# The last 30 expert rows of v: all through TensorE's diagonal matmuls, none added by VectorE into the residual

## The chip, the cores and the metric

The kernel runs on one core of one Trainium2 chip. The metric is the device time of one launch in microseconds (us), lower is better. The engines are TensorE (PE in the profile, its weight loads are PEld), VectorE (DVE), ScalarE (ACT), GpSimd (POOL) and SyncE (SP). The profile is of one execution on the same core.

## The reference, cut to what matters

The program is three layers long: a convolution mixer, a sparse-attention mixer, and a third block that ends in a mixture of 16,384 tiny experts. The change lies in the last part of that third block. For each of 512 tokens and 8 heads, 16 experts are picked. Each has a row in `peer_u` (dotted with the token) and a row in `peer_v` (added with a weight into the token's output).

```python
def peer_ffn(h, w_q, sub_keys, u, v):
    ...
    g = jax.nn.softmax(top_s, axis=-1)
    def one_block(args):
        xb, ib, gb = args
        ue = jnp.take(u, ib, axis=0)
        a = jnp.einsum('thkd,td->thk', ue, xb, preferred_element_type=jnp.float32)
        w = jax.nn.gelu(a) * gb
        ve = jnp.take(v, ib, axis=0)
        return jnp.einsum('thk,thkd->td', w.astype(ve.dtype), ve)
...
x = x + peer_ffn(rmsnorm(x, norm_ffn[i]), peer_wq[i], peer_subkeys[i], peer_u[i], peer_v[i])
g_ple = jax.nn.sigmoid(rmsnorm(x, norm_ple[i]) @ ple_gate[i])
x = x + g_ple * (p[i] @ ple_proj[i])
```

All data is f32. The last two lines are the closing stage, called ple below: it needs the finished sum over all expert rows of its tokens.

## The kernel before, in words

The 512 tokens are four blocks of 128, one token to a partition. A block and a head make a group; there are 32 groups of 16 picks, so 512 picks. One pick (a "row" below) is one gather of 128 different rows of 1024 f32, 0.5 MB, by GpSimd's indirect DMA: one from `peer_u` (line 1567, tile G) and one from `peer_v` (line 1583, tiles H and XT). Both kinds go out on GpSimd's one queue, in program order: u and v gathers take turns until the u gathers end, and then the v gathers left over (480 to 511) follow one another. The groups are ordered so that block 3's come last; rows 384 and above, and so all that the change touches, belong to block 3.

**u.** VectorE dots each u row with the token's normalized input (line 2246). When the 16 dots of a group are there it makes the weights together with ScalarE: `activated` (lines 2160 to 2162), `weigh` on ScalarE (lines 1433 and 1434), `weighted` (lines 2168 to 2171).

**v through TensorE.** For row v ScalarE scales the identity by the 128 weights of that pick (`diagonal`, line 1446), into one of 8 diagonal buffers in MK. TensorE multiplies this diagonal by the gathered row, in two halves of 512 columns, and accumulates in the block's two PSUM banks (`expert_row`, line 1017). The profile has four matmul records for such a row, two for each half. The end of the second half raises `v_done`. ScalarE's order puts `weigh` of the last group ahead of the diagonal of row 480.

**v through VectorE.** A row for which `by_vector(v)` is true (line 170) skips the diagonal and TensorE. VectorE adds weight times row into the residual X (`add_row`, line 2179), once it is through with the last group's weights, and raises `v_added`. With V_LATE = 482 these are rows 482, 485, ..., 509: 10 of the last 30.

**Buffers of v.** From row 96 on there are 8 row buffers, used in turn: 4 in H (`v_loaded0` to `3`) and 4 in XT (`v_loaded4` to `7`). The gather of row v waits until row v - 8 has been consumed, on `v_done` or on `v_added`, whichever engine consumed it (lines 1577 to 1581). `by_tensor(v)` and `vector_rows(v)` count the rows up to v that each engine takes; the waits and the diagonal's buffer number follow from them.

**The closing stage of block 3.** `ple_sum` on VectorE waits for `v_done` of row 511 and adds the two banks to X (line 2187). TensorE transposes (line 1079), ScalarE and VectorE scale and copy (lines 1455, 2193), TensorE runs the gate's matmuls (line 1091), ScalarE takes the sigmoid (line 1463), VectorE multiplies and adds (lines 2211, 2212), and SyncE stores (line 514). The projection of block 3 (line 1106, 8 records) stands in TensorE's order ahead of row 499.

Of the kernel before, what the change touches and what calls it, by code (L numbers as in the profile page):

```python
# [47 lines left out]
V_LATE = PICKS - 30  # L48
# [120 lines left out]

def by_vector(v):  # L170

    return v >= V_LATE and v % 3 == 2


def vector_rows(v):

    return sum(by_vector(a) for a in range(v + 1))


def by_tensor(v):  # L180

    return sum(not by_vector(a) for a in range(v + 1))
# [7 lines left out]
def program(nc, x, xT, mem, wstream, fmvec, rows, norm_rows, consts, levels, subkeys, pT, proj, peer_u, peer_v, out):  # L190
    with ExitStack() as ctx:
# [327 lines left out]
        def _(pe):  # L519
# [486 lines left out]
            def expert_row(v):  # L1006
                if by_vector(v):
                    return
                n, k = v // PEER_K, v % PEER_K
                b = group(n)[0]  # L1010
                if v == 0:
                    pe.wait_ge(tail_free, made)
                at, uses = v_place(v)
                pe.wait_ge(diag_full, by_tensor(v))
                pe.wait_ge(v_loaded[at], 16 * uses)
                for half in range(2):
                    mm = pe.matmul(ps[2 * b + half][:, :], DG[by_tensor(v - 1) % DIAG_RING], VB[at][:, half * T:(half + 1) * T],  # L1017
                                   start=(n == FIRST[b] and k == 0), stop=(n == LAST[b] and k == PEER_K - 1),
                                   skip_group_check=True)
                mm.then_inc(v_done, 1)  # L1020
# [1328 lines left out]
```

## Time and profile before

| what | value |
|---|---|
| time, median of 3 runs | 3289.33 us |
| the three runs | 3283.68, 3296.66, 3289.33 us |
| span of the profiled execution | 3278.9 us |
| TensorE busy | 2812.3 us, 86% |
| VectorE busy | 1829.2 us, 56% |
| GpSimd busy | 1273.9 us, 39% |
| mean granted TensorE clock | 0.967 |

The profiled execution's own time, with launch and end around the span, is not listed apart; its span lies 10.4 us below the median of the runs. The rows' gathers fill the last part of the span: in 16 of the last 17 of the page's 40 slices the DMA engines move 345 to 387 GB/s, and in the last 15 slices TensorE is busy 6 to 8 tenths.

### The profile page before, as it was taken

How to read it: one execution, taken by the hardware profiler on the slowest of the kernel's cores; microseconds unless marked ns; L12 is line 12 of the kernel's file. 1: busy time of each engine (PE TensorE's matmuls, PEld its weight loads, DVE VectorE, ACT ScalarE, POOL GpSimd, SP SyncE). 2: the span in 40 equal slices, each digit the busy share in tenths (PEclk: the TensorE clock that was granted, in tenths of full speed). 3: DMA queues.
4: the chain of work that ended last, by engine and by line, in shares of the span. 5: the costliest groups of instructions: out<-in, count | busy, mean ns of one | idle time of the engine just before them, and what ended most of it. 6: DMA issues, size and time to landing. Idle time of an engine off the chain costs nothing.

```text
span 3278.9 us, 26326 instructions
## 1 busy us (share of the span) xinstructions
PE 2812.3 (86%) x7932; PEld 1338.4 (41%) x7932; DVE 1829.2 (56%) x4230; ACT 652.2 (20%) x1556; POOL 1273.9 (39%) x1113
## 2 busy tenths in 40 slices
PE   9999999998889899988898889777768786777778
PEld 4455445454554444555555334322223232222323
DVE  4989502058751322267529666576666666666643
ACT  1114301022320112344401111111111111111111
POOL 0520000000000000022104767777777777777774
PEclk9999999999999999999999999999989999999999
DMA  4221122220112111001216999999999999999996
GB/s 179 77 103 52 64 77 77 77 77 26 51 40 77 67 69 51 26 30 49 90 65 216 366 371 368 371 387 373 345 361 371 363 353 367 372 366 352 368 386 244
DMA packets 161469, 665.89 MB, mean 203 GB/s; under 512 B 17856, under 2 KB 18240, under 8 KB 154304
## 3 DMA queue, kind: packets, MB, share of 16 engines
q0 software_dynamic: 147456, 536.94, 43.9%
q1 hardware_dynamic: 12032, 117.43, 9.8%
q10 hardware_dynamic: 1856, 10.00, 0.8%
q8 instruction: 61, 1.00, 0.1%
q14 instruction: 64, 0.52, 0.0%
HBM read 662.19 MB, written 2.10 MB: 203 GB/s over the span
## 4 chain that ended last, share of the span: by engine, by line
PE 54%; POOL 18%; issue 9%; DVE 9%; DMA 7%; ACT 2%; another core or an unknown queue 0%; DVEq 0%; ACTq 0%; POOLq 0%; SPq 0%
PE ps L537 13%; PE ps L1017 8%; POOL G L1567 8%; PE ps L652 6%; POOL H L1583 5%; POOL XT L1583 4%; PE ps L589 4%; PE ps L882 3%; DMA XT<-peer_v,C 3%; DMA H<-peer_v,C 3%; PE ps L790 2%; PE ps L911 2%; PE ps L819 2%; DMA G<-peer_u,C 2%; PE ps L976 2%
## 5 line engine op out<-in xcount | busy, mean ns | idle before, releaser
L2246 DVE CUSTOM_DVE_ANT_0 G<-G,H 128x1024 f32<-128x1024 f32 x512 | 627.7, 1226 | 465.7 <-DMA G<-peer_u,C 396.0
L1017 PE MATMUL ps<-H,MK 128*128 128x512 f32 x1196 | 591.2, 623 | 190.3 <-DMA H<-peer_v,C 124.0
L1567 POOL DMA_INDIRECT G<-peer_u,C x512 | 540.3, 1055 | 302.9 <-issue 151.8
L537 PE MATMUL ps<-XT,W 128*128 128x512 f32 (+1 forms) x1344 | 543.0, 553 | 8.9 <-issue 6.5
L1017 PE MATMUL ps<-XT,MK 128*128 128x512 f32 x812 | 403.1, 629 | 130.6 <-DMA XT<-peer_v,C 80.3
L1017 PEld LDWEIGHTS ps<-H,MK 128*128 128x128 f32 x1196 | 218.6, 195 | 532.3 <-issue 476.0
L1583 POOL DMA_INDIRECT H<-peer_v,C x304 | 350.6, 1153 | 131.3 <-issue 71.8
L537 PEld LDWEIGHTS ps<-XT,W 128*128 128x128 f32 x1344 | 254.1, 190 | 294.2 <-issue 286.2
L1017 PEld LDWEIGHTS ps<-XT,MK 128*128 128x128 f32 x812 | 149.5, 197 | 381.1 <-issue 326.0
L1542 POOL COPY PR<-H 128x256 f32<-128x256 f32 x4 | 1.4, 392 | 781.2 <-DVE H L1871 781.2
L1446 ACT ACTIVATE MK<-C 128x128 f32<-128x128 f32 x502 | 175.0, 393 | 524.5 <-PE ps L1017 292.6
L1583 POOL DMA_INDIRECT XT<-peer_v,C x208 | 241.1, 1159 | 78.7 <-issue 48.5
L652 PE MATMUL ps<-W,Y 128*128 128x512 f32 x512 | 226.1, 603 | 13.1 <-DVE Y L1746 6.1
L589 PE MATMUL ps<-XT,W 128*128 128x512 f32 x448 | 220.5, 604 | 1.6 <-ACT G L1152 1.6
L1554 POOL TENSOR_TENSOR H<-H 128x256 f32<-128x256 f32 x56 | 47.6, 852 | 353.9 <-ACT H L1376 320.6
L1645 DVE SCALAR_TENSOR_TENSOR Y<-H,V,Y x240 | 165.3, 765 | 0.0
L652 PEld LDWEIGHTS ps<-W,Y 128*128 128x128 f32 x512 | 98.3, 193 | 140.3 <-issue 137.1
L1433 ACT ACTIVATE H<-C 128x16 f32<-128x16 f32 x32 | 6.9, 216 | 630.3 <-DVE H L2162 336.8
L1528 POOL TENSOR_TENSOR H<-H,SIG 128x512 f32 x12 | 73.5, 6125 | 111.9 <-ACT SIG L1212 108.9
L1755 DVE SCALAR_TENSOR_TENSOR X<-X,H 128x512 f32<-128x512 f32 x16 | 11.1, 691 | 181.9 <-ACT H L1137 181.9
L589 PEld LDWEIGHTS ps<-XT,W 128*128 128x128 f32 x448 | 80.6, 195 | 59.7 <-issue 55.7
L882 PE MATMUL ps<-W,XT 128*128 128x512 f32 x192 | 98.5, 622 | 0.3 <-issue 0.3
(296 smaller groups left out, 3121.3 us busy)
## 6 DMA issues: line engine op xcount, KB each, us to landing
W<-wstream SPq DMA_DIRECT2D x51, 2048.0 KB
G<-peer_u,C POOLq DMA_INDIRECT x512
H<-peer_v,C POOLq DMA_INDIRECT x304
XT<-peer_v,C POOLq DMA_INDIRECT x208
XT<-xT SPq DMA_DIRECT2D x8, 256.0 KB, 5.3
W<-wstream SPq DMA_DIRECT2D x8, 256.0 KB, 5.8
X<-x SPq DMA_DIRECT2D x1, 2048.0 KB, 19.0
SIG<-rows ACTq DMA_DIRECT2D x4, 512.0 KB, 6.4
```

What stands on the lines that cost most here:

```text
L537: mm = pe.matmul(b[:, 0:rhs[k].shape[-1]], w[:, k, m * P:(m + 1) * P], rhs[k], start=(k == 0), stop=(k == KD - 1))
L589: mm = pe.matmul(FILL_BANK[j % 2][:, :], w[:, k, m * P:(m + 1) * P], XT[:, k, :], start=(k == 0), stop=(k == KD - 1))
L652: mm = pe.matmul(ps[pos % 4][:, :], Y[:, (j * KD + k) * T + b * P:(j * KD + k) * T + (b + 1) * P], w[:, k, :], start=(j == 0 and k == 0), ...
L790: mm = pe.matmul(ps[p0 % 4][:, 0:n], XT[:, k, b * P:(b + 1) * P], w[:, k, 0:n], start=(k == 0), stop=(k == KD - 1))
L882: mm = pe.matmul(ring(pos)[:, :], XT[:, k, b * P:(b + 1) * P], w[:, k, :], start=(k == 0), stop=(k == KD - 1))
L1017: mm = pe.matmul(ps[2 * b + half][:, :], DG[by_tensor(v - 1) % DIAG_RING], VB[at][:, half * T:(half + 1) * T], start=(n == FIRST[b] and k ...
L1446: act.activation(DG[at % DIAG_RING], ident, ACT.Copy, scale=GW[:, v:v + 1]).then_inc(diag_full, 1)
L1528: pool.tensor_tensor(hrow(i * 4 + j, TAPS - 1, T), hrow(i * 4 + j, TAPS - 1, T), SIG[:, j, :], ALU.mult).then_inc(glu_done, 1)
L1567: pool.indirect_dma_start(UB[u % U_RING], None, peer_u, bass.IndirectOffsetOnAxis(ap=IDX[:, u:u + 1], axis=0)).then_inc(u_loaded[u % U_RIN ...
L1583: pool.indirect_dma_start(VB[at], None, peer_v, bass.IndirectOffsetOnAxis(ap=IDX[:, v:v + 1], axis=0)).then_inc(v_loaded[at], 16)
L1645: ins = dve.scalar_tensor_tensor(yt(c), hrow(c, k, T), V[:, ds(c * TAPS + (FM["conv_w"] + k), 1)], yt(c), ALU.mult, ALU.add)
L2246: dve.tensor_tensor_reduce(out=rows_u, in0=rows_u, in1=tm(H, 0, D, group(n)[0]), scale=1.0, scalar=0.0, op0=ALU.mult, op1=ALU.add, accum_o ...
```

## The change

`by_vector` returns False for every row. So `diagonal` and `expert_row` no longer skip any, `gather_v` always waits on `v_done`, the loop over `add_row` at the end of VectorE's program issues nothing, and `by_tensor(v)` is v + 1.

```diff
@@ -169,7 +169,7 @@
 
 def by_vector(v):
 
-    return v >= V_LATE and v % 3 == 2
+    return False
```

On TensorE the difference begins behind row 481. The names: ps6 and ps7 are block 3's two accumulators, H and XT hold gathered rows, MK the diagonals, and the number in `v_loaded` is the row buffer.

```order
 L1017 MATMUL ps6<-H,MK 128x512 [waits v_loaded1,diag_full]
 L1017 MATMUL ps7<-H,MK 128x512
+L1017 MATMUL ps6<-H,MK 128x512 [waits v_loaded2,diag_full]
+L1017 MATMUL ps7<-H,MK 128x512
 L1017 MATMUL ps6<-H,MK 128x512 [waits v_loaded3,diag_full]
 L1017 MATMUL ps7<-H,MK 128x512
 L1017 MATMUL ps6<-XT,MK 128x512 [waits v_loaded4,diag_full]
 L1017 MATMUL ps7<-XT,MK 128x512
+L1017 MATMUL ps6<-XT,MK 128x512 [waits v_loaded5,diag_full]
+L1017 MATMUL ps7<-XT,MK 128x512
```

Two matmuls are added for each of the 10 rows 482, 485, ..., 509, each pair in its place among the others; nothing else on TensorE changes order.

On VectorE, behind the last group's weights (line 2171), the adds into the residual X stood before the sum of block 3 (line 2187).

```order
 L2171 TENSOR_TENSOR C<-H 128x16 [waits dve_link]
-L2179 SCALAR_TENSOR_TENSOR X<-H,C,X 128x1024 [waits weights,v_loaded2]
-L2179 SCALAR_TENSOR_TENSOR X<-XT,C,X 128x1024 [waits weights,v_loaded5,v_added]
...
-L2187 TENSOR_TENSOR X<-X,ps 128x512 [waits v_done,v_added]
+L2187 TENSOR_TENSOR X<-X,ps 128x512 [waits v_done,weights]
 L2187 TENSOR_TENSOR X<-X,ps 128x512
```

All 10 adds are gone, and VectorE goes from the weights straight to the wait for TensorE's last row.

On GpSimd, at the end of its program, the gathers of v rows keep their order; what they wait for changes.

```order
-L1583 DMA H<-peer_v,C 128x1024 [waits v_done] x2
-L1583 DMA H<-peer_v,C 128x1024 [waits v_added]
-L1583 DMA H<-peer_v,C 128x1024 [waits v_done]
-L1583 DMA XT<-peer_v,C 128x1024 [waits v_done]
-L1583 DMA XT<-peer_v,C 128x1024 [waits v_added]
...
+L1583 DMA H<-peer_v,C 128x1024 [waits v_done] x4
+L1583 DMA XT<-peer_v,C 128x1024 [waits v_done] x4
```

The eight gathers of rows 490, 493, ..., 511, whose buffers VectorE freed, now wait for TensorE too.

## Rows read from the trace of the kernel before

**Rows 1.** The page's head and the chain that ended last, shares by engine.
```profile
span 3278.9 us, 26326 instructions
...
PE 54%; POOL 18%; issue 9%; DVE 9%; DMA 7%; ACT 2%; another core or an unknown queue 0%; DVEq 0%; ACTq 0%; POOLq 0%; SPq 0%
```

**Rows 2.** The chain's end in order of time: start us, us, what.
```profile
3208.70 1.23 DVE G L2246
...
3247.15 6.47 DMA XT<-peer_v,C
3253.76 3.69 PE ps L1017 x8
3257.54 0.70 DVE X L2187
...
3260.26 13.99 PE ps L1091 x32
```

**Rows 3.** TensorE's timeline from row 480 to 511: start, us, records, idle before.
```profile
3211.36 5.42 PE L1017 MATMUL ps<-H,MK 128*128 128x512 f32 x12 [0.22 <-ACT MK L1446]
3216.61 5.58 PE L1017 MATMUL ps<-XT,MK 128*128 128x512 f32 x12
3222.57 3.67 PE L1017 MATMUL ps<-H,MK 128*128 128x512 f32 x8 [0.38 <-issue]
...
3237.07 3.60 PE L1106 MATMUL ps<-MK,PR 128*128 128x512 f32 x8
...
3253.76 3.67 PE L1017 MATMUL ps<-XT,MK 128*128 128x512 f32 x8 [1.08 <-DMA XT<-peer_v,C]
```

**Rows 4.** GpSimd's timeline, gathers of v rows.
```profile
3203.49 0.94 POOL L1583 DMA_INDIRECT H<-peer_v,C  x1 [0.30 <-issue]
...
3215.38 0.93 POOL L1583 DMA_INDIRECT H<-peer_v,C  x1 [0.30 <-PE ps L1017]
...
3217.86 1.18 POOL L1583 DMA_INDIRECT H<-peer_v,C  x1 [0.30 <-issue]
...
3221.83 1.50 POOL L1583 DMA_INDIRECT XT<-peer_v,C  x1 [0.30 <-issue]
3223.64 0.94 POOL L1583 DMA_INDIRECT XT<-peer_v,C  x1 [0.30 <-issue]
...
3248.39 0.99 POOL L1583 DMA_INDIRECT XT<-peer_v,C  x1 [0.30 <-issue]
```

**Rows 5.** VectorE's timeline: adds of row 482, 488 and 509, then the sum.
```profile
3212.98 1.28 DVE L2179 SCALAR_TENSOR_TENSOR X<-H,C,X 128x1024 f32<-128x1024 f32 x1 [1.08 <-DMA H<-peer_v,C]
...
3221.24 1.28 DVE L2179 SCALAR_TENSOR_TENSOR X<-H,C,X 128x1024 f32<-128x1024 f32 x1 [3.01 <-DMA H<-peer_v,C]
...
3252.47 1.28 DVE L2179 SCALAR_TENSOR_TENSOR X<-XT,C,X 128x1024 f32<-128x1024 f32 x1 [3.89 <-DMA XT<-peer_v,C]
3257.54 1.29 DVE L2187 TENSOR_TENSOR X<-X,ps 128x512 f32<-128x512 f32 x2 [3.79 <-PE ps L1017]
```

**Rows 6.** TensorE's timeline, v rows one behind another without a gap.
```profile
3039.13 7.03 PE L1017 MATMUL ps<-H,MK 128*128 128x512 f32 x16
3046.00 7.03 PE L1017 MATMUL ps<-XT,MK 128*128 128x512 f32 x16
```

**Rows 7.** ScalarE's timeline, the first nine diagonals from row 480 on, then one more.
```profile
3210.92 2.86 ACT L1446 ACTIVATE MK<-C 128x128 f32<-128x128 f32 x9
3215.09 0.40 ACT L1446 ACTIVATE MK<-C 128x128 f32<-128x128 f32 x1 [1.31 <-PE ps L1017]
```

**Rows 8.** Stretches: length, busy PE PEld DVE ACT POOL, clock, DMA share, GB/s.
```profile
1200.00:1400.00 200.00, 198.80 (x716) 97.94 (x714) 43.47 (x138) 58.07 (x124) 0.00 (x0) 1.00 0.12 44
3035.00:3058.00 23.00, 23.00 (x55) 9.91 (x53) 14.70 (x39) 6.28 (x13) 18.12 (x17) 1.00 0.96 346
3205.00:3211.36 6.36, 4.00 (x6) 1.18 (x5) 3.27 (x9) 0.76 (x5) 5.14 (x5) 0.54 0.98 360
3211.36:3257.43 46.07, 42.88 (x96) 17.61 (x96) 13.31 (x13) 7.60 (x21) 29.30 (x27) 1.00 0.90 331
```

## The prediction

> **What bounds the kernel now.** I read the chain of waits first. As a whole it is mixed [rows 1], so I went to its end in order of time. The reader is to see there that VectorE's last u dot at 3208.7 releases the last weights, and that a gather ends the wait for the last rows, that of row 511, whose data land 6.5 us after its start, and TensorE does the last two rows and hands over to the sum on VectorE [rows 2]. No add is on this chain. So in the last stage, from TensorE's start of row 480 at 3211.36 to its end at 3257.43 [rows 3], the supply of rows ends last, and TensorE follows at its heels.
>
> Next TensorE's timeline of that stage [rows 3]. The reader is to see how little air it has: of 46.07 us it is busy 42.88, with 96 records: 88 for 22 v rows and 8 for block 3's projection, at a granted clock of 1.00 [rows 8]. Then GpSimd: its last gather, of row 511, starts at 3248.39, and counted back from it the gather of row 480 is the one at 3203.49; 31 steps in 44.90 us, 1.45 us a row [rows 4]. Last the cost of a row on TensorE when nothing holds it back: 16 records of four rows start at 3039.13 and the next 16 at 3046.00, so 6.87 us for 16, 0.429 us a record, 1.717 us a row [rows 6], at clock 1.00, the 2.4 GHz level [rows 8].
>
> These two rates are the whole case. Rows arrive every 1.45 us and TensorE needs 1.72 us for one. Before, TensorE has 22 of 32 and keeps up; with all 32 it cannot.
>
> **The change part by part.**
>
> *Added to TensorE.* 10 rows x 4 records = 40 records x 0.429 = 17.2 us [rows 6]. All lie between row 480 and row 511, on the engine whose last record releases the closing stage.
>
> *Air taken from TensorE.* The 96 records of before need 96 x 0.429 = 41.2 us. They took 46.07, so 4.9 us is waiting, restart after a wait and the tail of the last record. The first 12 records took 5.25 us for 5.15 (3211.36 to 3216.61), and a record ends some 0.16 us behind the time at which a next one could start (7.03 against 6.87) [rows 3, 6]; these 0.26 us stay. The other 4.6 us are waits for rows on their way. They go if all rows land before TensorE wants them.
>
> *Do they?* With all 32 rows TensorE starts row 480 + i at about 3211.46 + 1.717 i, plus 3.43 from row 499 on. The tightest is the first added one: row 482 is wanted at 3214.9, and VectorE's add of it began at 3212.98 [rows 5], so it had landed 1.9 us early. Row 488 is wanted at 3225.2 and had landed by 3221.24 [rows 5]. The slack grows by some 0.27 us a row until buffers are short. From there gather v waits for TensorE to finish row v - 8. Gather 490 waits for row 482, done by 3216.7 (start 3214.9 plus 1.7, and some 0.2 for the signal), and started at 3217.86 anyway; gather 493 waits for row 485, done at about 3221.9, against 3221.83 before [rows 4]. So from gather 493 on TensorE's pace rules the gathers. The buffer then has 7 row times, 12.0 us, until the next use, and a gather from start to landing took 5.9 us (row 488, from 3215.38 to the add at 3221.24 [rows 4, 5]) to 6.5 us (row 511 [rows 2]). 5.5 us are left. The wait of gathers 490, 493, ..., 511 is thereby longer than before, and behind each on GpSimd's queue stand only later v gathers, which the same slack covers. No air remains, and this term is -4.6 us. Its two ends: 0 if every wait stayed, -4.6 if all go. I take -4.6, since every landing that I can place is early.
>
> *ScalarE.* Ten more diagonals of 0.40 us [rows 7], made up to 7 rows ahead of TensorE. 8 of the 32 are made at once, each further one when a row ends, so 0.40 us in every 1.72. Hidden. If that cover were gone, each row would show some of the 0.40 us; rows in which TensorE ran without a gap had the same ring of diagonals [rows 6], so the term is 0, with 10 x 0.4 = 4 us as its upper end.
>
> *Taken from VectorE.* 10 adds of 1.28 us, 12.8 us of work in which VectorE was waiting for data most of the time: 3.0 us before the second one shown, 3.9 before the last. The last add ended at 3253.75, and the sum then waited 3.79 us more for TensorE [rows 5]. So the adds were beside the path, and taking them away returns 0. What is late next is what was late already: TensorE.
>
> *The closing stage.* Nothing moves in it. From TensorE's end at 3257.43 to the end of the span are 21.5 us, a chain that starts from the last `v_done` [rows 1, 2]. It shifts as a whole. The projection (8 records, 3.43 us) stays in its place [rows 3]. Ahead of row 482 no instruction differs, so everything up to 3211.36 costs the same.
>
> *Sum.* +17.2 - 4.6 = +12.6 us. TensorE's last row ends at 3270.0 and the span is 3291.5 us. Checked from the other side: 136 records x 0.429 = 58.4, +0.26, from 3211.36, gives 3270.0. The span of the profile lies 10.4 us below the median of the runs; what lies around it does not change, so 3289.33 + 12.6 = 3302 us, slower by 0.38%.
>
> **A rule on GpSimd's gathers.** Gathers that start while a VectorE add runs take longer: the one at 3221.83 took 1.50 us during the add of 3221.24 to 3222.52, the next 0.94 [rows 4, 5]. Without the adds a gather could start every 0.94 + 0.30 = 1.24 us instead of 1.45. The Trainium skill, in "SBUF — State Buffer", section "Who interferes with whom", says that a VectorE instruction with two SBUF inputs contends only with what GpSimd reads, and holds, as an inference, that making descriptors needs the write side; by it the adds should not hold the gathers up and their end frees nothing. This trace speaks rather against it. By the rule or by the row, TensorE's 1.72 us a row is longer than either interval, and the sum is the same; what hangs on it is the chance of the faster rival.
>
> **The rivals.**
>
> *The supply still bounds.* If the added rows brought as many waits as the old ones had, the whole 17.2 us would show: 3306.5 us, +0.52%. For it: the last two rows of before did start behind a 1.08 us wait for a gather [rows 3], and landings that wander by 5 us would bring such waits back. Against it: rows arrive at 1.45 us against 1.72, and the buffers hold 8.
>
> *The clock falls.* From 3205 to 3211.36, where TensorE had waited, it was granted 0.54, mostly the 1.2 GHz level, and had 1.00 again from 3211.36 on [rows 8]. If the denser stage fell to the lower level for 6 us, TensorE would lose 3 us: 3305 us. Against it: 200 us at 99% busy ran at 1.00 [rows 8].
>
> *Faster, since the adds slowed the gathers.* Place: GpSimd from gather 481 on. At 1.24 us a step gather 511 starts at 3203.49 + 31 x 1.24 = 3241.9, lands 6.5 us later at 3248.4, and two rows (3.67 us) end at 3252.1: 5.3 us earlier than now, 3284 us. It decides only from the point at which TensorE does a row in under (3252.1 - 3211.36 - 3.43) / 32 = 1.17 us. No gapless row in the trace is under 1.72.
>
> *The change does nothing that can be measured in place.* If TensorE's waits were 17 us and not 4.6, it would be 0: 3289 us. The 42.88 us of busy time in 46.07 exclude it almost.
>
> **How the numbers follow.** The forecast has 0.84, the supply rival 0.08, the clock 0.04, the faster one 0.02, nothing 0.02. About 0.5%, 16.4 us here, is what a measurement of this kernel can tell from no change; the three runs before lie 13 us apart. With +12.6 the forecast is within that bound, but 3.8 us from its edge: with a scatter of about 6 us between two medians, 0.24 of its chance passes the edge (0.20). The supply rival gives 0.05 more, the clock 0.02. Slower 0.27, faster 0.02, same 0.71. The range: 3302 less 8 for scatter, 3294, to the supply rival's 3306.5 and 4 more for scatter, 3310.5, say 3311.
>
> **What would show it.** In the profile after: line 1017 has 128 records from row 480 on, with no gap from there to row 511, except the projection; TensorE's last record ends 58.7 us after row 480's start; the chain's end names TensorE for the whole stretch and no gather; GpSimd waits for TensorE from gather 493 on, in steps of 1.72 us, each gather at 0.94 us; the closing stage again lasts 21.5 us. It would be wrong if TensorE's timeline showed waits on DMA between added rows, if a record took more than 0.43 us, or if row 480 started elsewhere than about 3211, which nothing in the change explains.

## The result and the profile after

The changed kernel is slower by a third of a per cent: 3295.09 us against 3283.11 us (medians of 13 runs each), ratio 1.0034 with a 95% interval of 1.0020 to 1.0049. That is 12.0 us between the medians, where 12.6 were forecast; the interval alone would allow 6.6 to 16.1 us. Ratios leave out two executions in a slower state, 4264.5 us in e7 and 8096.1 us in e8. The absolute 3302 us lies 7 us too high, because the three runs of before that the forecast started from had a median 6 us above that of all 13.

The chain of waits of the changed kernel, its end in order of time: start us, us, what.

```profile
3197.21 5.79 DMA H<-peer_v,C
3203.00 1.69 issue
3204.69 32.88 PE ps L1017 x76
3237.58 3.43 PE ps L1106 x8
3241.01 22.33 PE ps L1017 x52
...
3263.79 0.70 DVE X L2187
...
3266.51 13.99 PE ps L1091 x32
```

Where before had a gather and its landing ahead of the last two rows [rows 2], TensorE alone carries the chain from its start of row 480 to the end of row 511. TensorE's timeline of the same stage, which answers to [rows 3]:

```profile
3204.69 7.13 PE L1017 MATMUL ps<-H,MK 128*128 128x512 f32 x16 [1.95 <-issue]
3211.66 7.03 PE L1017 MATMUL ps<-XT,MK 128*128 128x512 f32 x16
...
3237.41 3.60 PE L1106 MATMUL ps<-MK,PR 128*128 128x512 f32 x8
3240.85 1.88 PE L1017 MATMUL ps<-H,MK 128*128 128x512 f32 x4
...
3256.30 7.03 PE L1017 MATMUL ps<-XT,MK 128*128 128x512 f32 x16
```

No row behind the first shows idle time before it. The stretch as a whole (length, busy PE PEld DVE ACT POOL, clock, DMA share, GB/s), beside [rows 8]:

```profile
3204.69:3263.33 58.64, 58.63 (x136) 25.76 (x136) 0.47 (x3) 11.51 (x31) 25.04 (x27) 1.00 0.73 260
```

136 records in 58.64 us against 96 in 46.07 us: 12.57 us more. The DMA share falls from 0.90 to 0.73, since gathers now wait for buffers. GpSimd's timeline, gathers of rows 489, 490, 496, 497, 506 and 507, beside [rows 4]:

```profile
3209.36 0.94 POOL L1583 DMA_INDIRECT H<-peer_v,C  x1 [0.30 <-issue]
3212.90 0.94 POOL L1583 DMA_INDIRECT H<-peer_v,C  x1 [2.60 <-PE ps L1017]
...
3220.68 0.94 POOL L1583 DMA_INDIRECT H<-peer_v,C  x1 [0.62 <-issue]
3222.40 0.94 POOL L1583 DMA_INDIRECT H<-peer_v,C  x1 [0.78 <-issue]
...
3237.85 0.94 POOL L1583 DMA_INDIRECT H<-peer_v,C  x1 [0.78 <-PE ps L1017]
3243.00 0.94 POOL L1583 DMA_INDIRECT H<-peer_v,C  x1 [4.21 <-PE ps L1017]
```

From row 496 on they come every 1.72 us, TensorE's pace, and the pause ahead of gather 507, which waits for row 499, is the projection. VectorE has nothing to do between its weights and the sum:

```profile
3263.79 1.28 DVE L2187 TENSOR_TENSOR X<-X,ps 128x512 f32<-128x512 f32 x2 [58.55 <-PE ps L1017]
```

The span grew by only 6.2 us (3285.1 against 3278.9): in this execution row 480 started at 3204.69, 6.7 us earlier than at 3211.36 [rows 3], on instructions that are the same in both. Such scatter of the long gather stage is why the stage, and not the span, is compared from here on. "The stage" is the time from TensorE's start of row 480 to its end of row 511. The start moves in identical kernels as well: before had it at 3211.36 and 3169.69 (e5), the changed kernel at 3204.69 and 3147.80 (e6).

### The profile page after: what moved, and what is told of

Read it like the earlier page. It is cut to its first block, busy times and chain, and to the rows that moved or that the text cites. A ratio compares the mean times of both kernels' runs of the same rounds, so it can differ in the third digit from the quotient of the medians.

```text
span 3285.1 us, 26406 instructions
## 1 busy us (share of the span) xinstructions
PE 2835.6 (86%) x7972; PEld 1351.3 (41%) x7972; DVE 1816.5 (55%) x4220; ACT 656.2 (20%) x1566; POOL 1257.7 (38%) x1113
## 4 chain that ended last, share of the span: by engine, by line
PE 57%; POOL 15%; issue 9%; DVE 9%; DMA 9%; ACT 2%; another core or an unknown queue 0%; DVEq 0%; ACTq 0%; SPq 0%; POOLq 0%
PE ps L537 13%; PE ps L1017 11%; POOL G L1567 7%; PE ps L652 6%; POOL H L1583 5%; DMA H<-peer_v,C 4%; PE ps L589 4%; POOL XT L1583 3%; PE ps L882 3%; DMA XT<-peer_v,C 2%; PE ps L790 2%; PE ps L911 2%; PE ps L819 2%; DMA G<-peer_u,C 2%; PE ps L976 2%
## 5 line engine op out<-in xcount | busy, mean ns | idle before, releaser
L1017 PE MATMUL ps<-H,MK 128*128 128x512 f32 x1216 | 601.4, 624 | 168.3 <-DMA H<-peer_v,C 98.8
L1017 PE MATMUL ps<-XT,MK 128*128 128x512 f32 x832 | 415.1, 633 | 125.8 <-DMA XT<-peer_v,C 81.0
(294 smaller groups left out, 3209.9 us busy)
```

## The experiments

The runs went to chips of different pace: the kernel before had medians of 3229 us (the first four), 3225 us (the next four) and 3290 us (the last three). e1 to e4 ran on one chip, e5 to e8 on a second, e9 to e11 on a third. Ratios are against before on the same chip. Each stage is that of one profiled execution. With 32 rows on TensorE it repeats to a hundredth; where TensorE waits for gathers, a single delay moves it by 1 us and more (e10 and e11 below), so differences of that size count there only as far as the single instructions bear them out.

| run | rows on TensorE | stage us | gathers over 1.1 us, of 32 | ratio, 95% interval |
|---|---|---|---|---|
| before, first profile | 22 | 46.07 | 10 | 1 |
| changed, first profile | 32 | 58.64 | 2 | 1.0034 (1.0020 to 1.0049) |
| e1 | 27 | 50.06 | 2 | 1.0024 (1.0007 to 1.0042) |
| e2 | 18 | 43.05 | 7 | 0.9991 (0.9970 to 1.0011) |
| e3 | 22 | 42.98 | 0 | 0.9982 (0.9965 to 0.9999) |
| e4 | 22 | 42.68 | 0 | 0.9991 (0.9968 to 1.0014) |
| e5, before again | 22 | 46.74 | 5 | 1.0002 (0.9981 to 1.0022) |
| e6, changed again | 32 | 58.64 | 0 | 1.0047 (1.0026 to 1.0069) |
| e7 | 32 | 58.63 | 23 | 1.0028 (1.0009 to 1.0048) |
| e8 | 18 | 41.88 | 0 | 0.9996 (0.9972 to 1.0020) |
| e9 | 32 | 55.21 | 1 | 1.0020 (1.0005 to 1.0036) |
| e10 | 22 | 44.63 | 2 | 0.9989 (0.9974 to 1.0004) |
| e11 | 18 | 46.00 | 0 | 0.9993 (0.9977 to 1.0008) |

### Half of the change (e1)

```diff
-    return v >= V_LATE and v % 3 == 2
+    return v >= V_LATE and v % 6 == 2
```

> VectorE adds only 5 of the last 30 rows (482, 488, ..., 506); TensorE has 27 of the rows 480 to 511. The stage is TensorE's time from its start of row 480 to its end of row 511: 46.07 us before, 58.64 us in the changed kernel. Theory (TensorE's 1.717 us a row rules once it has more rows than the gathers supply in time): 27 x 1.717 + 3.43 + 0.26 = 50.1 us, no wait for a gather of more than 0.5 us, time of the kernel +4 us against before (ratio 1.0012). Rival (the waits of before stay, each added row costs its whole 1.717 us): 46.07 + 5 x 1.717 = 54.7 us, +8.6 us.

The stage is 50.06 us, the forecast to a tenth. TensorE's timeline, start and end of the run of rows:

```profile
3145.40 5.42 PE L1017 MATMUL ps<-H,MK 128*128 128x512 f32 x12 [1.86 <-ACT MK L1446]
3150.66 7.03 PE L1017 MATMUL ps<-XT,MK 128*128 128x512 f32 x16
...
3188.43 7.03 PE L1017 MATMUL ps<-XT,MK 128*128 128x512 f32 x16
```

With 27 rows TensorE already runs without a wait. So the first five moved rows cost 3.99 us, what was left once the waits were used up, and the next five (50.06 to 58.64) cost 8.58 us, 1.716 each, the full price. The kernel's ratio came out above the forecast 1.0012, which its interval still holds. The interval holds the rival's +8.6 us (1.0027) too, so it is the stage that decides between them.

### Fewer rows on TensorE (e2)

```diff
-    return v >= V_LATE and v % 3 == 2
+    return v >= V_LATE and v % 2 == 0 and v != 496
```

> VectorE adds 14 of the last 30 rows (482, 484, ..., 510 without 496); TensorE has 18 of 32. The stage is TensorE's time from row 480 to row 511 (46.07 us before). Theory (before, the supply of rows rules, so taking rows from TensorE gives nothing back): no shorter than 45 us. If the adds also hold the gathers up, by some 0.5 us each, 4 more adds make it 2 us longer, 48 us; if the gathers' interval is set by the memory, 46 us. Rival (TensorE's count of rows rules before as well): 46.07 - 4 x 1.717 = 39.2 us, and the kernel 7 us faster.

43.05 us: below both of the theory's numbers and above the rival's. On another chip of about this pace before has 46.74 (e5), of which up to 1.7 us come from a stretch at the lower clock (below). So taking four rows from TensorE gives back some 2 to 3.7 us of stage, where 6.9 would be full price, and nothing that the timing can tell. Supply rules there, as claimed, but not as firmly.

### What the adds cost the gathers (e3, e4, e5)

e3 narrows each add to 16 columns:

```diff
-                dve.scalar_tensor_tensor(X[:, b, :], VB[at], GW[:, v:v + 1], X[:, b, :], ALU.mult, ALU.add
-                                         ).then_inc(v_added, 1)
+                dve.scalar_tensor_tensor(X[:, b, 0:16], VB[at][:, 0:16], GW[:, v:v + 1], X[:, b, 0:16],
+                                         ALU.mult, ALU.add).then_inc(v_added, 1)
```

> As before, but each of VectorE's 10 adds covers only the first 16 of 1024 columns (the other columns of these 10 rows are left out of the sum). Buffers are released as before. Theory that the adds hold GpSimd up: in before a gather beside an add took 1.2 to 1.7 us and the others 0.94; here all take 0.94 us, the interval of the last 31 gathers falls from 1.45 to about 1.25 to 1.3 us, TensorE waits no more, its stage falls from 46.07 us to 22 x 1.717 + 3.7 = 41.5 us, and the kernel is 4.5 us faster than before. Rival (the interval of 1.45 us is the memory's): durations and interval stay, the stage stays at 46 us, the same time as before.

e4 keeps the arithmetic and puts the sum into two free PSUM banks:

```diff
+                for half in range(2):
+                    cols = slice(half * T, (half + 1) * T)
+                    if vector_rows(v) == 1:
+                        ins = dve.tensor_scalar(ps[half][:, :], VB[at][:, cols], GW[:, v:v + 1], None, ALU.mult)
+                    else:
+                        ins = dve.scalar_tensor_tensor(ps[half][:, :], VB[at][:, cols], GW[:, v:v + 1],
+                                                       ps[half][:, :], ALU.mult, ALU.add)
+                ins.then_inc(v_added, 1)
...
+            for half in range(2):
+                cols = slice(half * T, (half + 1) * T)
+                ins = dve.tensor_tensor(X[:, NB - 1, cols], X[:, NB - 1, cols], ps[half][:, :], ALU.add)
+            ch.link(ins)
```

> As before, with all the arithmetic, but VectorE's 10 rows are accumulated in two PSUM banks that are free by then (two halves of 512 columns, one operand in SBUF and one in PSUM), and the banks are added to the residual once behind the last row. VectorE does more work than before. If what holds GpSimd up is an add with two SBUF operands: gathers take 0.94 us, interval 1.25 to 1.3 us, the stage (46.07 us before) becomes 41.5 us, 4.5 us faster than before. If any VectorE work on a full row holds GpSimd up: gathers beside it at 1.2 to 1.7 us, stage 46 to 47 us. If the memory sets the interval: 1.45 us and 46 us as well, whatever the adds are.

> The kernel before once more, with a profile, since the first four experiments ran on a chip on which every kernel is some 55 us faster than in the first profile. It gives the stage from TensorE's row 480 to row 511 and the gathers' durations where the experiments ran. Expected from the theory that adds hold gathers up: gathers beside an add take 1.2 to 1.9 us, the last 31 steps take more than the 42.1 us of the narrow adds, the stage is 44 to 46 us. If the adds cost nothing: the stage is 43 us, as with narrow adds. The ratio to before should be 1.000 within its interval, and shows what the timing can tell.

GpSimd's timeline around the second add, first in before again (e5), where the add runs from 3174.81 to 3176.09, then with sums in PSUM (e4), where VectorE's work on its second row runs from 3168.12 to 3169.53:

```profile
3175.36 1.54 POOL L1583 DMA_INDIRECT H<-peer_v,C  x1 [1.55 <-PE ps L1017]
3177.21 0.94 POOL L1583 DMA_INDIRECT H<-peer_v,C  x1 [0.30 <-issue]
```

```profile
3168.25 0.94 POOL L1583 DMA_INDIRECT H<-peer_v,C  x1 [0.30 <-issue]
3169.49 0.94 POOL L1583 DMA_INDIRECT H<-peer_v,C  x1 [0.30 <-issue]
```

No gather of the last 32 goes over 1.1 us in e3 or e4, against five in e5 and ten in the first profile. That VectorE is busy is not what matters, since e4 does more VectorE work than before (1.41 us a row). What does is where the add reads or writes: e4 moved both the second operand and the result from SBUF to PSUM (and works in halves), and no run keeps these apart. The stage is 4.1 us shorter in e4 than in e5. Not all of that is the adds': e5's first 12 records took 6.95 us where [rows 3] has 5.25, in a stretch at the lower clock (same columns as above):

```profile
3169.69:3174.00 4.31, 4.31 (x6) 1.83 (x7) 1.76 (x4) 2.40 (x8) 2.51 (x3) 0.61 1.03 411
```

Taking those 1.7 us off, I estimate the adds' share at 2.4 us (2.1 by e3). The gathers' own durations say much the same: those of rows 480 to 510 took 2.7 us more than 0.94 us each in e5, and 0.2 us more in e4. A pair at equal clock, 1.00, is e2 and e8 (below), 14 rows on VectorE with either kind of add, on two chips of about the same pace: 43.05 against 41.88 us, so 1.2 us. The 41.5 us that I had expected were missed by 1.2 to 1.5 us: a gather still came only every 1.36 us and not every 1.25 to 1.3, since gather 507 waited 3.0 us for row 499 behind the projection, and TensorE waited a little for rows 492, 495 and 498. In the time of the kernel e3 is faster by 0.2% (it leaves most of ten rows' sum out), and e4, which computes all, can't be told from before.

### The changed kernel again, and with adds beside it (e6, e7)

> The changed kernel once more on this chip. Theory: a stage of 58.6 us again, whatever the chip's gathers do, since TensorE's 32 rows and the projection fill it (136 records x 0.429 + 0.26); 12 to 15 us more than before's stage on this chip, ratio 1.004 to 1.005. Rival (the supply of rows has a share in it): a stage shorter by the 3 us by which supply-bound stages are shorter here, 55 to 56 us, ratio 1.003.

58.64 us, the same to a hundredth on a chip on which the whole kernel is 58 us faster, and 11.9 us more than before there (e5). The ratio of 1.0047 is at the upper side of the first measurement's interval.

e7 puts into the changed kernel, in the loop that had the adds:

```diff
             for v in range(V_LATE, PICKS):
-                if by_vector(v):
-                    add_row(v)
+                dve.wait_ge(v_done, v - 1)
+                ch.link(dve.scalar_tensor_tensor(UB[2], UB[0], GW[:, v:v + 1], UB[1], ALU.mult, ALU.add))
```

> The changed kernel with 30 adds of 128x1024 on VectorE beside the last 30 rows, on buffers that nothing else uses by then (two operands in SBUF, one add for each row that TensorE ends; their result is not used). Theory: gathers that fall beside an add take 1.2 to 1.9 us in place of 0.94, but a row is still issued every 1.717 us, since 1.9 + 0.3 is rare and the buffers hold 5.5 us of slack; stage 58.6 to 59.5 us and the time of the changed kernel, ratio 1.004. Rival (the changed kernel profits from the freed gathers, the supply rival of the prediction): the stage grows by 3 us or more, with waits for gathers between rows. If contention with VectorE were no cause of the long gathers: all stay at 0.94.

Two of VectorE's adds, then two gathers of GpSimd that run beside them:

```profile
3166.44 1.29 DVE L2257 SCALAR_TENSOR_TENSOR G<-G,C 128x1024 f32<-128x1024 f32 x1 [0.43 <-PE ps L1017]
3168.16 1.28 DVE L2257 SCALAR_TENSOR_TENSOR G<-G,C 128x1024 f32<-128x1024 f32 x1 [0.43 <-PE ps L1017]
```

```profile
3167.12 1.42 POOL L1583 DMA_INDIRECT XT<-peer_v,C  x1 [0.30 <-issue]
3168.84 1.41 POOL L1583 DMA_INDIRECT H<-peer_v,C  x1 [0.30 <-issue]
```

The adds make 23 of 32 gathers long, on buffers that have nothing to do with the gathers, and the stage stays at 58.63 us. 1.41 + 0.30 is 1.71 us, just inside TensorE's 1.717 us a row. Both statements hold at once: adds do slow gathers, and the changed kernel doesn't feel it.

### Towards a faster version (e8 to e11)

e8 is e4 with 14 rows on VectorE (the line of e2).

> All the arithmetic; VectorE takes 14 of the last 30 rows, accumulated in free PSUM banks, TensorE 18 of 32. Theory: gathers go unhindered at a step of 1.24 us, and TensorE's 18 rows (34.6 us) no longer delay them, so the supply alone sets the stage: 31 x 1.24 = 38.4 us from gather 480 to gather 511, less 8.0 us to the start of row 480, plus 6.4 us for landing and 2.0 us for row 511, 38.9 us; 4 us less than the 42.7 us of 22 rows on TensorE with the same adds; ratio to before 0.998. Rival (the memory does not deliver a row every 1.24 us): landings fall behind, stage 43 us as with 14 ordinary adds, ratio 0.999.

41.88 us, a miss of 3. GpSimd's timeline shows the place, the gathers of rows 506 and 507:

```profile
3177.45 0.94 POOL L1583 DMA_INDIRECT H<-peer_v,C  x1 [0.30 <-issue]
3181.10 0.94 POOL L1583 DMA_INDIRECT H<-peer_v,C  x1 [2.71 <-PE ps L1017]
```

Gather 507 waits for row 499, which stands behind the projection. From gather 480 to gather 511 are 41.7 us where 31 x 1.24 = 38.4 had been expected, and this pause, 2.4 us over the usual 0.30, is most of the difference. The last three runs move the projection:

```diff
-                    if v == (LAST_V[b] - 12 if b > 0 else LAST_V[b] + 36):
+                    if v == (LAST_V[b] - (42 if b == NB - 1 else 12) if b > 0 else LAST_V[b] + 36):
```

> The changed kernel with block 3's projection (8 records, 3.43 us) moved from ahead of row 499 to ahead of row 469, where TensorE waits some 0.6 us in each row. Theory (in the changed kernel every record between row 480 and 511 counts in full): stage 58.64 - 3.43 = 55.2 us, and if the waits of rows 469 to 479 take the projection in, the kernel is 3.4 us faster than the changed one: ratio to before about 1.003. Rival (the projection only fills time that the supply leaves): stage stays above 57 us.

55.21 us, as expected, and the price of a record in this stage is confirmed with work of another kind: 8 records, 3.43 us. Against before the ratio is 1.0020; against the changed kernel (1.0034 and 1.0047 in its two measurements) it is lower, but their intervals overlap.

> All the arithmetic: VectorE's 10 rows go to free PSUM banks, and the projection stands ahead of row 469. TensorE has 22 rows, 38.0 us without a wait. Theory: with the projection where it was, the gather of row 507 waited 2.7 us for row 499 behind it; now the gathers run at 1.24 us from row 489 on, the last starts 31.3 us after row 480's start and its row ends 8.2 us later: stage 39.5 us (42.7 with the projection in place, 46 to 47 in the kernel before), ratio 0.998. Rival (landings fall behind when gathers come every 1.24 us): 41 to 42 us.

> As the run with 14 rows in PSUM, with the projection ahead of row 469; TensorE has 18 rows. There the stage was 41.9 us and not 38.9 as I had expected, with a pause of the gathers ahead of row 507 behind the projection, from 3177.45 to 3181.10. Theory: that pause is the miss; without it 39.5 us, the same as with 22 rows on TensorE, since the supply alone sets it. Rival (the memory's pace): 41 to 42 us with waits for gathers spread over all rows.

Both missed, by 5 and 6.5 us. They ran on the slow chip. TensorE in e10 stands still for late data again, though no add disturbs the gathers:

```profile
3222.92 3.67 PE L1017 MATMUL ps<-XT,MK 128*128 128x512 f32 x8 [0.20 <-issue]
...
3235.47 1.95 PE L1017 MATMUL ps<-XT,MK 128*128 128x512 f32 x4 [0.97 <-DMA XT<-peer_v,C]
...
3240.09 3.67 PE L1017 MATMUL ps<-H,MK 128*128 128x512 f32 x8 [0.94 <-DMA H<-peer_v,C]
3243.85 3.67 PE L1017 MATMUL ps<-XT,MK 128*128 128x512 f32 x8
```

These are rows 486 and 487, row 495, rows 498 and 499, rows 501 and 502. It looks like the rival's picture, but the gathers had not been issued in time. GpSimd's gathers of rows 494, 495 and 510, then ScalarE's three diagonals from the one that needs row 487's buffer:

```profile
3226.44 0.94 POOL L1583 DMA_INDIRECT XT<-peer_v,C  x1 [0.30 <-issue]
3230.20 0.93 POOL L1583 DMA_INDIRECT XT<-peer_v,C  x1 [2.82 <-PE ps L1017]
...
3251.73 0.94 POOL L1583 DMA_INDIRECT XT<-peer_v,C  x1 [3.23 <-PE ps L1017]
```

```profile
3229.96 1.14 ACT L1446 ACTIVATE MK<-C 128x128 f32<-128x128 f32 x3 [4.57 <-PE ps L1017]
```

Gather 495 waits for row 487, whose records ended at 3226.59; ScalarE and GpSimd went on together, only 3.4 and 3.6 us later, though GpSimd had been idle since 3227.38. Gather 510 waits for row 502, which ended at 3247.52, 4.2 us before. Once issued, row 495 was there in 5.3 us and row 510 in 4.4, sooner than the 6.5 us of [rows 2]. The two pauses are 5.5 us over the usual 0.30, and two gathers beside VectorE's last u dots took 1.5 us over 0.94; together they account for the 45.5 us from gather 480 to gather 511, 7.1 more than 31 x 1.24. In e11 the like stands ahead of gathers 487, 503 and 504 (3.85, 1.25 and 2.61 us), and its first 12 records took 6.95 us, as in e5, in a stretch at a clock of 0.58, which makes up to 1.7 of its 46.00 us. Why TensorE's release came late is open, and so is whether the memory would deliver a row every 1.24 us. Ahead of gather 507 neither run has a pause, so moving the projection did remove e8's; that it wins time isn't shown, as e8 and e11 ran on different chips and other pauses came.

None of the versions that compute everything is faster than before beyond its interval; e10, at 0.9989 (0.9974 to 1.0004), comes nearest.

## Why the prediction was right, point by point

**TensorE's added records, +17.2 us.** Right. 40 records more in the profile, at 0.429 us; e1, e6 and e9 price rows and projection alike.

**The air, -4.6 us.** Right in size: the stage grew by 12.57 us. All of it went, and e1 shows that five rows use it up.

**ScalarE and the closing stage, 0.** Right. The diagonals ran beside the matmuls; from TensorE's end to the end of the span are 21.8 us, against 21.5 before.

**The adds, 0.** Right for this change, and too narrow as a statement. I priced them as VectorE's time beside the path. They were also a load on GpSimd, whose gathers were what TensorE waited for: an estimated 1.2 to 2.4 us of before's waits were of their making (e3 and e4 against e5, e8 against e2). The sum did not suffer, since it started from the 46.07 us that include them and ended at TensorE's own length, which doesn't depend on them (e7). The faster rival had the right mechanism, and its point of decision, a row on TensorE in under 1.17 us, was nowhere near.

**The rule on descriptors.** I had taken from the inference cited from the Trainium skill ("SBUF — State Buffer", "Who interferes with whom") that an add with two SBUF inputs should not hold the gathers up. The gathers are held up: 1.41 us against 0.94 in e7. But I had thought of the descriptors alone. A gather also reads its 128 row numbers from tile C in SBUF, so which of the two the add slows, the reading or the making of descriptors, no run here shows, and the inference itself is neither borne out nor refuted. The section's other half, that the second SBUF input is what contends, agrees with e4.

**Where gathers begin to follow TensorE.** I said from gather 493. In the profile gather 490 already waited 2.60 us, until 3212.90, though TensorE's records put the end of row 482 at 3209.9. ScalarE's diagonal of row 490 came late as well, at 3212.66. In e6 no such pause shows, and the gathers follow TensorE's 1.72 us from row 489 on. It is the late release of e10 once more; its cause is open, and the buffers hid it. That e6 begins at 489 and not at 493 has a plain reason: I took the gathers' times from before, where those of rows 482, 484 and 487 had been long (1.37, 1.84 and 1.54 us), and in e6 none is.

**The sign of row 480.** I had named a start of row 480 elsewhere than about 3211 as a sign of being wrong. It was at 3204.69. Identical kernels scatter by more, as said above, so the sign was badly chosen, and the sum, which goes by differences, doesn't use it.

**The supply and clock rivals.** The changed kernel shows neither: three executions of 58.64, 58.64 and 58.63 us, all at clock 1.00.

**The chances.** The result lies within 0.5%, as forecast at 0.71, and the second measurement, 1.0047, shows how near the edge it is.

## What to carry to other kernels

Ask of a stage which of two rates is the longer: here a row every 1.45 us from the gathers against 1.72 us on TensorE. Moving work onto the slower side costs full price as soon as its waits are used up, and the waits can be read off beforehand as length minus records times pitch. An engine off the path can still set the pace of the one on it, by what its operands hold up: look at the durations of the other engine's instructions while it runs, not only at who waits for whom. And where an engine waits for data, look when the transfer was issued before blaming the memory (e10).

## What the runs showed of the hardware that I had not expected

- An indirect gather's issue on GpSimd takes 0.94 us, and 1.41 us beside each of VectorE's adds of 128x1024 with two SBUF operands (e7), but 0.94 us beside the same arithmetic with one operand and the result in PSUM (e4, e8).
- TensorE's release of a row's buffers sometimes comes late. The gather that needs the buffer usually starts 0.3 us after the row's records (e8), but it started 3.0 us after them in the changed kernel (row 482), 3.6 and 4.2 us in e10 (rows 487 and 502), and for rows 482 and 487 ScalarE's next diagonal was as late. The cause is open, and no run shows whether it happens without the profiler.
- The same kernel takes 3225 to 3290 us depending on the chip. TensorE's stage does not change with it (58.64 us on both kinds); what the gathers supply does: from 2000 to 2400 us before moved 371 GB/s in the first profile and 392 in e5, the changed kernel 375 and 395 (e6).
